# Opening the third attention branch in one stage: the first queries projected between shared keys and values

## The chip, the cores and the metric

The kernel runs on one core of one Trainium2 chip. The metric is the device time of one execution in microseconds (us), as the median of several executions. Beside it stands one profiled execution, from which all rows of the trace come. TensorE (PE) multiplies matrices, VectorE (DVE) and ScalarE (ACT) work elementwise, GpSimd (POOL) does some elementwise work, and the sync engine (SP) issues most DMA transfers.

## The reference

Two blocks run one after the other on 512 tokens of 1024 features, in float32. The first is a transformer block and is not touched. The second has two layers with 256 context tokens beside the 512 latent ones. Each layer projects the normalised input with one wide matrix, runs three attention branches and merges them. The third branch is the one that matters here:

```python
def swa_heads(q, k, v, rope):
    q = q.reshape(b, n, SWA_HEADS, SWA_HD)        # 16 heads of 64
    k = k.reshape(b, n, SWA_KV_HEADS, SWA_HD)     # 4 shared heads of 64
    v = v.reshape(b, n, SWA_KV_HEADS, SWA_HD)
    if rope is not None:
        q = apply_rope(q, *rope)
        k = apply_rope(k, *rope)
    return q, k, v
...
    sq_l, sk_l, sv_l = swa_heads(sq_l, sk_l, sv_l, rope_hd)
    sq_c, sk_c, sv_c = swa_heads(sq_c, sk_c, sv_c, None)
    yc_l = swa_latent(sq_l, sk_l, sv_l, sk_c, sv_c, swa_sink)
```

Queries look at a window of 128 latent tokens to either side and at all context tokens, with a sink term in the softmax. Rope is applied to the latent tokens only. In layer 0 context queries are computed as well, in layer 1 they are not. Then each branch's output is gated and merged.

## The kernel before

Everything is kept feature-major in the on-chip memory: 128 features on the partitions, tokens along the free axis (512 latent, then 256 context). A projection of 128 output features is a *split* product. The weight tile (8 x 128 x 128 values) is loaded in two halves of 256 KB by SP (`load_split`), ScalarE rounds it to a high part (`act_high`, L582), VectorE computes the low part (`dve_low`, L592), and TensorE makes three products for each of 8 input tiles: high by high, high by low and low by high (`split_steps`, `pe_split`; all matrix products go through `mm` and carry line L596). One projection of all 768 tokens is 48 products, one of 512 tokens is 24. Two slots are used in turn for raw, high and low weights; counters on semaphores say which weight is ready. Weight loads are issued by SP in program order, each waiting until its slot's last low part is computed.

`plan()` lists the stages, and each engine goes through them in that order. Between stages each engine calls `fence`: it drains, raises its own fence counter, and waits for the other two engines' counters, unless the stage has a `follower` or is one of some exceptions. A layer of the second block is: norm, `pre`, first branch (`mla`), merge, second branch (`diff`), merge, `swapre`, third branch (`swa`), merge, `out`.

`swapre` opens the third branch. It projects the shared keys (two weights of 128 columns, four key heads) and values (two weights). After each key projection ScalarE (L2403) and VectorE (L2647) copy the results from the accumulator memory to `KB`. After each value projection VectorE copies them to `probs` (L2650). When all four are done, TensorE multiplies the four key tiles with a constant that swaps halves (`rot_hd`, one product each, shown as two records), and then transposes the values (L2251, 12 blocks). VectorE meanwhile turns the keys, four times three operations (`dve_rope`, L1304 to L1307), and then copies the turned values to `v` (L2658). Then comes a fence.

`swa` has 8 steps, one for each pair of query heads. A prologue projects the first pair's queries. ScalarE copies them to `qT` (L1247), SP swaps their halves with four small transfers (`sp_swap`, L447 and L448), GpSimd does the rope on them (`pool_rope`, L1314, L1315, L1317), ScalarE rounds queries and keys (`act_qk_high`, L1270, L1274), VectorE makes their low parts (`dve_qk_low`, L1291, L1295), and only then can TensorE make scores. In each step TensorE makes the scores in groups of two, and between the groups it makes *side* products: the gate projection of this step (`swa_z`) and the next pair's query projection. VectorE takes maxima (L875, L882), ScalarE exponentials (L854), TensorE transposes probabilities and multiplies them with the values, and VectorE scales the result. The next pair's queries pass through the same chain of copy, swap, rope and rounding while the step's values are made.

SP's order in `swa` is written out: the first query weight; then, for each step, the step's gate weight, the next query weight, and the swap of the step's queries.

## Time and profile before

| | us |
|---|---|
| median of 3 runs | 4010.91 |
| lowest and highest run | 4010.6 and 4015.4 |
| profiled execution, its own time | 4009.09 |
| its span, first to last instruction | 4007.3 |
| TensorE busy | 3683.3 |
| VectorE busy | 2044.5 |
| ScalarE busy | 1405.6 |
| GpSimd busy | 257.8 |

The span is what the trace covers, and the profiled execution's own time is 1.8 us longer. Busy times of matrix products are modelled from records, so they are a guide to where an engine works and not to how close it is to its peak. The mean granted clock of TensorE over the span is 0.962, where 1 is 2.4 GHz and 0.5 is 1.2 GHz. In a row of the timeline the first number is the start and the second the duration; a bracket at its end gives how long the engine had been idle and which instruction ended that.

### The profile page before, as it was taken

Reading aid. Unit: us, or ns where it says so; the run is one execution under the profiler, and the core shown is the slowest. Engines: PE = TensorE matmul, PEld = TensorE weight load, DVE = VectorE, ACT = ScalarE, POOL = GpSimd, SP = SyncE. Lnnn points to the kernel's source line nnn. Section 1 sums busy time; section 2 is a strip of 40 time slices with the busy share of each in tenths; the row PEclk is TensorE's granted clock in tenths of the full one; section 3 lists DMA queues with packets and bytes.
Section 4 is the critical chain, followed back from the end, with each engine's and each line's share of the span. In section 5 each row is a group of like instructions: output and inputs, shape, how many; then the busy total and the mean of one; then the engine's idle time right before and its main releaser. Section 6 shows DMA issues by size and latency. Waiting matters only on the chain.

```text
span 4007.3 us, 55652 instructions
## 1 busy us (share of the span) xinstructions
PE 3683.3 (92%) x20467; PEld 2856.3 (71%) x20467; DVE 2044.5 (51%) x3404; ACT 1405.6 (35%) x2502; POOL 257.8 (6%) x196
## 2 busy tenths in 40 slices
PE   5998989999899999999797999989999999798998
PEld 3665778877667787777586777876667777576676
DVE  3565355554445524777623555244552667534644
ACT  2443233323233313444412444122332444414532
POOL 0000000000011001111000110000110112001100
PEclk8999999999899999999898999999999999899999
DMA  7453335542111121211121111211113222121122
GB/s 256 143 144 83 92 102 164 163 136 79 38 29 28 38 63 48 52 47 44 33 62 43 35 40 46 63 53 37 37 39 87 58 65 52 50 74 48 40 73 77
DMA packets 502208, 286.94 MB, mean 72 GB/s; under 512 B 43753, under 2 KB 481093, under 8 KB 502062
## 3 DMA queue, kind: packets, MB, share of 16 engines
q1 hardware_dynamic: 481010, 263.63, 23.5%
q10 hardware_dynamic: 21052, 21.33, 1.7%
q8 instruction: 96, 1.57, 0.2%
q14 instruction: 50, 0.41, 0.0%
HBM read 269.05 MB, written 10.32 MB: 70 GB/s over the span
## 4 chain that ended last, share of the span: by engine, by line
issue 90%; PE 4%; POOL 3%; POOLq 2%; DVE 1%; DVEq 0%; ACT 0%; ACTq 0%
PE ps L596 3%; POOLq L1316 2%; POOL qT L1315 2%; POOL qT L1317 1%; POOL y_and_merged L1315 0%; DVEq L2687 0%; DVE probs L875 0%; PE ps L1022 0%; POOLq L208 0%; DVE y_and_merged L2664 0%; PE ps L2258 0%; DVE y_low L2483 0%; DVE w_low L592 0%; POOL y_and_merged L1317 0%; DVE probs L1928 0%
## 5 line engine op out<-in xcount | busy, mean ns | idle before, releaser
L596 PE MATMUL ps<-h_high,w_high 128*128 128x512 f32 (+1 forms) x3432 | 1287.9, 375 | 75.2 <-DVE w_low L592 24.7
L596 PE MATMUL ps<-h_low,w_high 128*128 128x512 f32 (+1 forms) x3432 | 1252.1, 365 | 0.0
L596 PE MATMUL ps<-h_high,w_low 128*128 128x512 f32 (+1 forms) x3432 | 1248.9, 364 | 0.0
L596 PEld LDWEIGHTS ps<-h_high,w_high 128*128 128x128 f32 x3432 | 655.4, 191 | 238.9 <-issue 97.4
L592 DVE TENSOR_TENSOR w_low<-w_raw,w_high 128x1024 fp32r<-128x1024 f32 x374 | 456.1, 1220 | 629.9 <-ACT w_high L582 607.0
L596 PEld LDWEIGHTS ps<-h_high,w_low 128*128 128x128 f32 x3432 | 656.0, 191 | 104.0
L596 PEld LDWEIGHTS ps<-h_low,w_high 128*128 128x128 f32 x3432 | 657.4, 192 | 92.8 <-issue 1.7
L582 ACT ACTIVATE w_high<-w_raw 128x1024 fp32r<-128x1024 f32 x374 | 387.7, 1037 | 604.6 <-PE ps L596 489.6
L854 ACT ACTIVATE probs<-ps,neg_max 128x768 f32<-128x768 f32 (+1 forms) x240 | 194.5, 814 | 430.2 <-DVE neg_max L886 430.1
L596 PE MATMUL ps<-probsT,v 128*128 128x512 f32 (+4 forms) x736 | 287.3, 560 | 13.5 <-DVE probsT L1085 8.6
L886 DVE TENSOR_REDUCE neg_max<-ps 128x1 f32<-128x768 f32 (+1 forms) x240 | 196.6, 847 | 167.6 <-PE ps L596 156.8
L596 PE MATMUL ps<-k_high,q_high 64*128 64x256 f32 (+4 forms) x784 | 184.5, 394 | 101.6 <-ACT probs L854 30.5
L596 PE MATMUL ps<-y_high,w_high 128*128 128x512 f32 (+1 forms) x640 | 231.5, 362 | 10.1 <-DVE w_low L592 9.2
L596 PE MATMUL ps<-y_low,w_high 128*128 128x512 f32 (+1 forms) x640 | 230.9, 361 | 0.0
L596 PE MATMUL ps<-y_high,w_low 128*128 128x512 f32 (+1 forms) x640 | 230.5, 360 | 0.0
L596 PEld LDWEIGHTS ps<-k_high,q_high 64*128 64x128 f32 (+1 forms) x784 | 91.1, 191 | 172.9 <-ACT probs L854 38.3
L854 ACT ACTIVATE probs<-probs,neg_max 128x512 f32<-128x512 f32 (+1 forms) x192 | 145.6, 758 | 179.4 <-DVE neg_max L878 129.7
L971 PEld LDWEIGHTS ps<-ident,probs 128*128 128x128 f32 x832 | 103.0, 143 | 106.2 <-issue 85.9
L2317 ACT ACTIVATE probs<-ps 128x512 f32<-128x512 f32 x88 | 44.8, 538 | 335.1 <-PE ps L596 335.1
L596 PE MATMUL ps<-y_and_merged 128*128 128x128 f32 (+4 forms) x656 | 153.3, 385 | 8.9 <-DVE y_and_merged L2096 4.6
L1085 DVE COPY probsT<-ps 128x512 f32<-128x512 f32 x112 | 73.2, 654 | 164.1 <-PE ps L971 163.9
L596 PE MATMUL ps<-k_low,q_high 64*128 64x256 f32 (+4 forms) x784 | 156.0, 330 | 0.0
(235 smaller groups left out, 4154.9 us busy)
## 6 DMA issues: line engine op xcount, KB each, us to landing
w_raw<-in_w_in SPq DMA_DIRECT2D x436, 256.0 KB, 3.2
y_and_merged<-in_w_mod SPq DMA_DIRECT2D x96, 256.0 KB, 3.2
w_raw<-in_w_branch SPq DMA_DIRECT2D x96, 256.0 KB, 3.0
w_raw<-in_w_up SPq DMA_DIRECT2D x88, 256.0 KB, 4.3
y_and_merged<-in_w_ada SPq DMA_DIRECT2D x64, 256.0 KB, 3.4
w_raw<-in_w_out SPq DMA_DIRECT2D x48, 256.0 KB, 3.0
w_raw<-in_w_down SPq DMA_DIRECT2D x44, 256.0 KB, 3.0
y_and_merged<-in_w_ada SPq DMA_DIRECT2D x4, 2048.0 KB, 19.7
```

Source lines behind the costliest of these rows:

```text
L582: act.activation(WR[:, k, 0:nk], WRAW[:, k, 0:nk], ACT.Copy).then_inc(s_high, 1)
L592: nc.vector.tensor_tensor(WL[:, k, 0:nk], WRAW[:, k, 0:nk], WR[:, k, 0:nk].bitcast(F32), ALU.subtract).then_inc(s_low, 1)
L596: return nc.tensor.matmul(*a, **kw)
L854: act.activation(it["dst"], src, ACT.Exp, bias=NM[:, idx:idx + 1], accum_out=SL[:, idx:idx + 1]).then_inc(S["exped"], 1)
L886: v.tensor_reduce(NM[:, idx:idx + 1], src, AXX, ALU.max, negate=True).then_inc(S["maxed"], 1)
L971: last = nc.tensor.transpose(PS[:, b:b + 128], tile, ident[:, :])
L1085: nc.vector.tensor_copy(PT[:, which, 0:m], PS[:, b:b + m]).then_inc(S["pt_dve"], 1)
L1315: g.tensor_tensor(x, x, cos, ALU.mult)
L1316: g.drain()
L1317: g.tensor_tensor(x, x, swapped, ALU.add).then_inc(S["roped"], 1)
L2317: last = act.activation(d, p, ACT.Tanh, scale=0.5)
```

## The change

`swapre` gets the third branch as its follower. It projects keys, keys, queries, values, values, instead of keys, keys, values, values, so the first pair's query projection moves from the prologue of `swa` into it. The four key turns are made in two pairs: the products of the first pair stand behind the second key projection, those of the second pair behind the query projection. Their temporary moves, since the swap of the queries now writes the old place. The values use the accumulator banks in another order. The first pair's queries are copied, swapped, turned and rounded inside this stage, and the prologue of `swa` is gone. Because there is a follower, no engine waits at the fence between the two stages. Two semaphores are new: `k_roped`, on which ScalarE waits before it rounds the first keys, and `v_turned`, on which TensorE waits before the first gate projection. SP now loads the first gate weight and swaps the first queries, and then, for each further step, loads the query weight, loads the gate weight and swaps. The number of products, copies and transfers is the same. The same edit removes `prologue()` from TensorE's, ScalarE's and VectorE's part of `swa` (one of the three is shown), and `dve_rope` takes its temporary and its semaphore as arguments.

```diff
@@ -134,8 +134,8 @@
         st += [Stage("merge", name="merge", r=1, subs=1, ctx=cq, l=l)]
-        st += [Stage("swapre", **com)]
-        st += [Stage("units", name="swa", n=8, nh=2, nn=0, subs=1, items=2 * ni, chunks=nc, unroll=1, **com)]
+        swa = Stage("units", name="swa", n=8, nh=2, nn=0, subs=1, items=2 * ni, chunks=nc, unroll=1, **com)
+        st += [Stage("swapre", follower=swa, **com), swa]
         st += [Stage("merge", name="merge", r=2, subs=1, ctx=cq, l=l)]
...
@@ -168,6 +168,9 @@
             n, subs = s["n"], s["subs"]
+            if s["name"] == "swa":
+                s.base["h"] -= 1
+                now["h"] -= 1
             add(s, h=n * s["nh"], n=n * s["nn"], scores=n * subs * s["items"], maxed=n * subs * s["items"],
...
@@ -196,7 +199,7 @@
         elif k == "swapre":
-            add(s, h=4, mm_ev=4, k_out=2, rope_mm=4, roped=4, vt_mm=2)
+            add(s, h=5, mm_ev=4, k_out=2, rope_mm=4, k_roped=4, vt_mm=2, v_turned=2)
     totals = dict(now)
...
@@ -516,13 +519,12 @@
-                        load_split(sp, s, t, 2, 1, cols(win2[l], i * 128 + C_Z + 2048))
                         load_split(sp, s, t, 2, 2, cols(win2[l], i * 128 + (C_SQ + 128)))
-                        sp_swap(sp, s, t, 1, 0)
-                    load_split(sp, s, 0, 2, 0, cols(win2[l], C_SQ))
+                        load_split(sp, s, t, 2, 3, cols(win2[l], i * 128 + (C_Z + 2048 + 128)))
+                        sp_swap(sp, s, t, 1, 1)
+                    load_split(sp, s, 0, 2, 1, cols(win2[l], C_Z + 2048))
+                    sp_swap(sp, s, 0, 1, 0)
                     repeat(sp, 7, 1, body)
-                    load_split(sp, s, 7, 2, 1, cols(win2[l], 7 * 128 + C_Z + 2048))
-                    sp_swap(sp, s, 7, 1, 0)
             elif k == "merge":
...
@@ -561,7 +563,7 @@
             elif k == "swapre":
-                for j, c in enumerate((C_SK, C_SK + 128, C_SV, C_SV + 128)):
+                for j, c in enumerate((C_SK, C_SK + 128, C_SQ, C_SV, C_SV + 128)):
                     load_split(sp, s, 0, 0, j, cols(win2[l], c))
...
@@ -1266,6 +1268,9 @@
             act.wait_ge(S["roped"], cnt(s, "roped", t, s["unroll"] * m, (u + 1) * m))
+            if name == "swa" and i == 0:
+                act.wait_ge(S["k_roped"], s.base["k_roped"])
             rows = slice(0, 96) if name == "mla" else slice(0, 128)
...
@@ -1536,6 +1540,9 @@
                     pe.wait_ge(S["z_ev"], cnt(s, "z_ev", t, 1, u))
+                else:
+                    pe.wait_ge(S["v_turned"], s.base["v_turned"])
                 yield from split_steps(pe, s, t, 2, 1, 128, tgroups(2, s["cq"]))
...
@@ -1649,7 +1656,6 @@
             if name == "swa":
-                prologue()
                 for i in range(7):
...
@@ -2234,22 +2238,27 @@
             elif k == "swapre":
-                for j in range(4):
-                    if j >= 2:
-                        pe.wait_ge(S["mm_ev"], s.base["mm_ev"] + 8 + j - 1)
-                        pe.wait_ge(S["k_out"], s.base["k_out"] + j - 1)
-                    pe_split(pe, s, 0, 0, j, 128, tgroups(2 * (j % 2), True))
-                for g in range(4):
-                    if g == 0:
-                        pe.wait_ge(S["mm_ev"], s.base["mm_ev"] + 8 + 4)
-                    mm(bank(4 + g), TAB["rot_hd"][:, :], KB[:, g, 0:LAT], start=True, stop=True).then_inc(S["rope_mm"], 1)
+                def keys_turned(pair):
+                    pe.wait_ge(S["mm_ev"], s.base["mm_ev"] + 8 + pair + 1)
+                    pe.wait_ge(S["k_out"], s.base["k_out"] + pair + 1)
+                    for g in (2 * pair, 2 * pair + 1):
+                        mm(bank(4 + g), TAB["rot_hd"][:, :], KB[:, g, 0:LAT], start=True, stop=True).then_inc(S["rope_mm"], 1)
+                pe_split(pe, s, 0, 0, 0, 128, tgroups(0, True))
+                pe_split(pe, s, 0, 0, 1, 128, tgroups(2, True))
+                keys_turned(0)
+                pe_split(pe, s, 0, 0, 2, 128, tgroups(0, s["cq"]))
+                keys_turned(1)
+                pe_split(pe, s, 0, 0, 3, 128, tgroups(2, True))
+                pe.wait_ge(S["rope_in"], s["follower"].base["rope_in"] + 1)
+                pe_split(pe, s, 0, 0, 4, 128, tgroups(0, True))
                 for e in range(2):
+                    pe.wait_ge(S["mm_ev"], s.base["mm_ev"] + 8 + 3 + e)
                     for tt in range(6):
-                        last = nc.tensor.transpose(PS[:, 1024 * e + 128 * tt:1024 * e + 128 * tt + 128],
-                                                   PP[:, TOK * e + 128 * tt:TOK * e + 128 * tt + 128], ident[:, :])
+                        last = nc.tensor.transpose(bank(2 - 2 * e, 128, 128 * tt), PP[:, TOK * e + 128 * tt:TOK * e + 128 * tt + 128], ident[:, :])
                     last.then_inc(S["vt_mm"], 1)
...
@@ -2402,6 +2411,13 @@
                         last.then_inc(S["k_out"], 1)
+                    if j == 2:
+                        act.wait_ge(s_h, s.base["h"] + 3)
+                        for d, p in evac_cols(s, 0, Q, s["cq"]):
+                            last = act.activation(d, p, ACT.Copy, scale=0.125)
+                        last.then_inc(S["rope_in"], 1)
+                act_qk_high(act, s["follower"], 0, 0, 0)
...
@@ -2630,32 +2646,53 @@
                 v.drain()
-                dve_rope(dve, s, 0, 0, 1, Q[0:96, 0:LAT], 96, 2, TAB["cos_mla"][:, :], TAB["sin_mla"][:, :])
+                dve_rope(dve, s, 0, 0, 1, Q[0:96, 0:LAT], 96, 2, TAB["cos_mla"][:, :], TAB["sin_mla"][:, :],
+                         PP[0:96, 4608:4608 + LAT], "roped")
                 v.tensor_copy(KH[64:96, :], Q[64:96, :])
                 v.drain()
                 v.tensor_tensor(KL[64:96, :], Q[64:96, :], KH[64:96, :].bitcast(F32), ALU.subtract)
                 dve_latent_inverse(dve, s, 1)
                 dve_latent(dve, s, 1)
             elif k == "swapre":
-                for j in range(4):
-                    dve_low(dve, s, 0, 0, j + 1)
+                def keys(j):
                     dve.wait_ge(s_h, s.base["h"] + j + 1)
-                    b = 1024 * (j % 2)
-                    if j < 2:
-                        for e in range(2):
-                            last = v.tensor_copy(KB[64 * e:64 * e + 64, 2 * j + 1, :], PS[64:128, b:b + TOK])
-                        last.then_inc(S["mm_ev"], 1)
-                    else:
-                        v.tensor_copy(PP[:, TOK * (j - 2):TOK * (j - 1)], PS[:, b:b + TOK]).then_inc(S["mm_ev"], 1)
-                dve.wait_ge(S["k_out"], s.base["k_out"] + 2)
-                v.drain()
-                for g in range(4):
-                    dve_rope(dve, s, g, 0, 1, KB[:, g, 0:LAT], 128, 4 + g, TAB["cos_hd"][:, :], TAB["sin_hd"][:, :])
+                    b = 1024 * j
+                    for e in range(2):
+                        last = v.tensor_copy(KB[64 * e:64 * e + 64, 2 * j + 1, :], PS[64:128, b:b + TOK])
+                    last.then_inc(S["mm_ev"], 1)
+                def turn_keys(pair):
+                    dve.wait_ge(S["k_out"], s.base["k_out"] + pair + 1)
+                    v.drain()
+                    for g in (2 * pair, 2 * pair + 1):
+                        dve_rope(dve, s, g, 0, 1, KB[:, g, 0:LAT], 128, 4 + g, TAB["cos_hd"][:, :], TAB["sin_hd"][:, :],
+                                 PP[:, 2 * TOK:2 * TOK + LAT], "k_roped")
+                def values(e):
+                    dve.wait_ge(s_h, s.base["h"] + 4 + e)
+                    b = 1024 - 1024 * e
+                    v.tensor_copy(PP[:, TOK * e:TOK * e + TOK], PS[:, b:b + TOK]).then_inc(S["mm_ev"], 1)
+                dve_low(dve, s, 0, 0, 1)
+                keys(0)
+                dve_low(dve, s, 0, 0, 2)
+                keys(1)
+                dve_low(dve, s, 0, 0, 3)
+                turn_keys(0)
+                dve_low(dve, s, 0, 0, 4)
+                turn_keys(1)
+                values(0)
+                dve_low(dve, s, 0, 0, 5)
+                dve_qk_low(dve, s["follower"], 0, 0, 0)
+                values(1)
                 for e in range(2):
                     dve.wait_ge(S["vt_mm"], s.base["vt_mm"] + e + 1)
-                    v.tensor_copy(VB[:, :, 128 * e:128 * e + 128], PS[:, 1024 * e:1024 * e + TOK].rearrange("p (a d) -> p a d", d=128))
+                    b = 1024 - 1024 * e
+                    v.tensor_copy(VB[:, :, 128 * e:128 * e + 128], PS[:, b:b + TOK].rearrange("p (a d) -> p a d", d=128)).then_inc(S["v_turned"], 1)
             elif k == "store":
```

## Rows read from the trace of the kernel before

**Rows 1.** The page, parts 1 and 6 (median us to landing last)

```profile
PE 3683.3 (92%) x20467; PEld 2856.3 (71%) x20467; DVE 2044.5 (51%) x3404; ACT 1405.6 (35%) x2502; POOL 257.8 (6%) x196
...
w_raw<-in_w_in SPq DMA_DIRECT2D x436, 256.0 KB, 3.2
```

**Rows 2.** Timeline of TensorE, opening in layer 0

```profile
2117.51 0.47 PE L596 MATMUL ps<-h_high,w_high 128*128 128x512 f32 x1 [2.64 <-DVEq L2687]
...
2152.16 3.27 PE L596 MATMUL ps<-y_and_merged,rot_hd 128*128 128x512 f32 x7 [1.05 <-DVE probs L2650]
...
2155.70 1.47 PE L2251 MATMUL ps<-ident,probs 128*128 128x128 f32 x12
...
2163.89 0.76 PE L596 MATMUL ps<-h_high,w_high 128*128 128x512 f32 x1 [6.71 <-DVEq L2687]
...
2186.47 0.58 PE L596 MATMUL ps<-k_high,q_high 64*128 64x256 f32 x2 [12.22 <-DVE k_low L1295]
```

**Rows 3.** Timeline of TensorE, a merge's projection and the opening in layer 1

```profile
3547.82 0.39 PE L596 MATMUL ps<-h_high,w_high 128*128 128x512 f32 x1
...
3553.26 0.39 PE L596 MATMUL ps<-y_high,w_high 128*128 128x512 f32 x1
...
3560.90 0.47 PE L596 MATMUL ps<-h_high,w_high 128*128 128x512 f32 x1 [2.04 <-DVEq L2687]
...
3595.55 3.70 PE L596 MATMUL ps<-y_and_merged,rot_hd 128*128 128x512 f32 x8 [1.05 <-DVE probs L2650]
...
3607.27 0.76 PE L596 MATMUL ps<-h_high,w_high 128*128 128x512 f32 x1 [6.71 <-DVEq L2687]
...
3626.50 0.58 PE L596 MATMUL ps<-k_high,q_high 64*128 64x256 f32 x2 [11.53 <-DVE k_low L1295]
```

**Rows 4.** Stretches: PE, PEld, DVE, ACT, POOL, clock, DMA share, GB/s

```profile
2117.40:2151.00 33.60, 33.49 (x192) 29.60 (x192) 9.70 (x9) 7.47 (x8) 0.00 (x0) 1.00 0.24 64
...
2163.80:2174.30 10.50, 10.35 (x48) 8.75 (x48) 1.23 (x1) 1.08 (x2) 0.00 (x0) 0.82 0.00 0
...
2186.40:2190.00 3.60, 3.54 (x17) 2.93 (x18) 1.71 (x8) 0.85 (x3) 0.00 (x0) 0.50 0.02 5
```

**Rows 5.** Timeline of VectorE, layer 0

```profile
2153.33 0.69 DVE L1304 TENSOR_TENSOR y_and_merged<-y_and_merged,cos_hd 128x512 f32<-128x512 f32 x1 [1.22 <-PE ps L596]
...
2161.93 1.82 DVE L2658 COPY v<-ps 128x768 f32<-128x768 f32 x2
```

**Rows 6.** Timeline, the first queries of layer 0

```profile
2174.28 0.87 ACT L1247 ACTIVATE qT<-ps 128x512 f32<-128x512 f32 x2 [9.35 <-PE ps L596]
...
2179.06 1.26 POOL L1314 TENSOR_TENSOR probs<-probs,sin_hd 128x512 f32<-128x512 f32 x1 [266.67 <-DMA probs<-qT]
...
2182.97 0.84 ACT L1270 ACTIVATE q_high<-qT 128x768 fp32r<-128x768 f32 x1 [7.83 <-POOL qT L1317]
...
2185.46 0.95 DVE L1295 TENSOR_TENSOR k_low<-y_and_merged,k_high 128x768 fp32r<-128x768 f32 x1
```

**Rows 7.** Timeline, steps of the branch in layer 0

```profile
2216.83 1.27 POOL L1314 TENSOR_TENSOR probs<-probs,sin_hd 128x512 f32<-128x512 f32 x1 [33.89 <-DMA probs<-qT]
...
2261.96 0.39 PE L596 MATMUL ps<-k_high,q_high 64*128 64x256 f32 x2
...
2290.09 1.27 POOL L1314 TENSOR_TENSOR probs<-probs,sin_hd 128x512 f32<-128x512 f32 x1 [33.10 <-DMA probs<-qT]
```

**Rows 8.** Timeline, second step of the branch in layer 1

```profile
3648.47 0.95 SPq L372 DMA_DIRECT2D w_raw<-in_w_in  x2
...
3653.91 1.04 ACT L582 ACTIVATE w_high<-w_raw 128x1024 fp32r<-128x1024 f32 x1
...
3657.46 0.72 ACT L854 ACTIVATE probs<-probs,neg_max 128x512 f32<-128x512 f32 x1 [2.50 <-DVE neg_max L878]
```

**Rows 9.** Timeline, VectorE beside GpSimd in the second branch

```profile
1730.38 1.94 DVE L592 TENSOR_TENSOR w_low<-w_raw,w_high 128x1024 fp32r<-128x1024 f32 x1
...
1731.19 2.28 POOL L1315 TENSOR_TENSOR qT<-qT,cos_hd 128x512 f32<-128x512 f32 x1
```

More of the change, by code:

```diff
@@ L148, in plan @@
     keys = ("h n square added square_mm rstd scaled high low_row lat_sq lat_ss lat_rs lat_ri lat_sp lat_n rinv spread fin down_ev x_t mm_ev rope_in rope_mm roped q_mm k_mm k_out q_out kv_ev kv_low vt_in vt_mm v_ev z_ev tanh swap_q swap_k z_scaled scores maxed exped normed "
-            "pt_act pt_dve rl_mm transposed o_done o_sq o_ss o_rs y bias merged up_ev gelu f_high f_low y_low y_high y_round m_high m_low out_ev ctx_in mod_copy mod_sum qk_high qk_low").split()
+            "k_roped v_turned pt_act pt_dve rl_mm transposed o_done o_sq o_ss o_rs y bias merged up_ev gelu f_high f_low y_low y_high y_round m_high m_low out_ev ctx_in mod_copy mod_sum qk_high qk_low").split()
     for k in keys:
@@ L1296, in dve_qk_low, with dve_rope @@
             last.then_inc(S["qk_low"], 1)
-        def dve_rope(dve, s, key_off, t, per, x, rows, b, cos, sin):
+        def dve_rope(dve, s, key_off, t, per, x, rows, b, cos, sin, tmp, done):
             dve.wait_ge(S["rope_mm"], cnt(s, "rope_mm", t, per, key_off + 1))
             v = nc.vector
-            tmp = PP[0:rows, 4608:4608 + LAT]
             v.tensor_tensor(x, x, cos, ALU.mult)
@@ L1306, in dve_rope @@
             v.drain()
-            v.tensor_tensor(x, x, tmp, ALU.add).then_inc(S["roped"], 1)
+            v.tensor_tensor(x, x, tmp, ALU.add).then_inc(S[done], 1)
             v.drain()
@@ L1768, in act_units @@
             if name == "swa":
-                prologue()
                 for i in range(7):
@@ L1856, in dve_units @@
             if name == "swa":
-                prologue()
                 for i in range(7):
@@ L2395, in act_stage @@
             elif k == "swapre":
-                for j in range(4):
+                for j in range(5):
                     act_high(act, s, 0, 0, j + 1)
```

1 line of the change is left out of this document (removed).

## The prediction

> **What bounds the kernel now.** I read the page first. TensorE is busy 92% of the span [rows 1], so time can only be won where it stands still or runs at the lower of its two clock levels. The timeline of TensorE then gives the two openings of the third branch, one per layer [rows 2, 3]. The first number of a row is its start and the bracket is the idle time before it, with its releaser. In layer 0 TensorE starts the first key projection at 2117.51, waits 1.05 us for VectorE's eviction of the last values, runs the rope products and the twelve transposes, waits 6.71 us at the fence, projects the first queries, waits 12.22 us for `k_low`, and starts the first scores at 2186.47. Layer 1 has the same picture with 1.05, 6.71 and 11.53 us. These six waits are 39.3 us together. The stretch view adds the clock: while the first queries are projected the granted clock is 0.82, and in the 3.6 us from 2186.40 it is 0.50, which is 1.2 GHz [rows 4]. In the 6.71 us VectorE makes four key turns from 2153.33 to 2161.93 (8.60 us, so 2.15 each), then two value copies of 1.82 us together [rows 5]. The first queries have a chain of their own [rows 6]: eviction at 2174.28, four copies by the DMA queue, GpSimd from 2179.06, ScalarE's rounding at 2182.97, VectorE's last `k_low` at 2185.46 for 0.95 us. It is a chain of small steps in which TensorE does nothing.
>
> **What the change does to TensorE's path, layer 0.** Before, from the first key product to the first score: 2186.47 - 2117.51 = 68.96 us [rows 2]. After, the same stretch is this sum.
> - Five projections instead of four ahead of the transposes. Four took until 2152.16 - 1.05 = 2151.11, so 33.60 us, 8.40 each. Five are 42.00 us. All stand back to back.
> - Eight rope records: 2155.70 - 2152.16 = 3.54 us, now in two halves of 1.77, with no wait. The first half needs the first keys' evictions, which ran while the second keys were projected, and the second half needs evictions that run beside the query projection.
> - The tail. Six transposes of the first values take 1.47 / 2 = 0.74 us, inside the 1.05 us that the last values' eviction takes. The other six follow, 0.74. So 1.05 + 0.74 = 1.79 us after the last projection.
> - The seam into the first scores. The stage has a follower, so the fence is passed with a drain and no wait. No row shows a drain alone. Below it is bounded by nothing, above by the 2.64 us of a whole fence at this stage's entry [rows 2]. A drain must only empty TensorE's own queue, so I take 0.2 us.
>
> Sum 42.00 + 3.54 + 1.79 + 0.20 = 47.53, against 68.96: 21.43 us won.
>
> **Layer 1.** Before: 3626.50 - 3560.90 = 65.60 us [rows 3]. Here the queries have 512 columns and no context. A projection of that size takes 3553.26 - 3547.82 = 5.44 us for its 24 products at the high clock, where it took 7.7 us after the fence. After: 4 x 8.40 + 5.44 + 3.54 + 1.79 + 0.20 = 44.57. Won: 21.03 us.
>
> **The clock after the opening.** The first step of the branch starts at 1.2 GHz. From the first score to GpSimd's next rope it takes 2216.83 - 2186.47 = 30.36 us, and the third step, which does the same work, takes 2290.09 - 2261.96 = 28.13 us [rows 2, 7]. After the change TensorE comes to the first scores out of 42 us of products. The 2.64 us of idleness at the entry left the granted clock at 1.00, 2.4 GHz, in the 33.6 us behind it [rows 4]. So 2.23 us a layer, 4.46 for both. I use layer 0's difference for layer 1 too.
>
> **What the sum rests on: who must be in time.** Let T be the end of the query projection.
> - The queries' chain. Eviction to the end of GpSimd's work is 2182.97 - 2174.28 = 8.7 us [rows 6], so it ends at T + 8.7. The values' first projection ends at T + 1.77 + 8.40 = T + 10.2. ScalarE rounds the next weight first, so `q_high` starts at about T + 11.2, and from `q_high` to `k_low`'s end before was 2186.41 - 2182.97 = 3.4 us, which gives T + 14.6. VectorE evicts the second values behind `k_low`, and these end at T + 18.6. So `k_low` has 4.0 us to spare, and GpSimd 2.5 us more ahead of `q_high`.
> - The keys' turns. VectorE turns two keys (4.3 us) while the queries are projected and two in the first values' projection, after one weight split at about T + 3.4, so they end by T + 7.8. That is ahead of the values' eviction at T + 10.2. This work was the larger part of the 6.71 us. It is hidden only as long as a projection is longer than it.
> - The new wait on `v_turned` stands ahead of the first gate projection, because that writes the banks that the value copies read. Behind it on TensorE are all side products of the first step and the second pair of scores. VectorE's copies start when the last eviction ends and end 1.05 + 1.82 = 2.87 us after the last projection. The first scores start at 1.99. The wait is at most 0.88 us a layer and at least nothing. One pair of scores fills most of that gap, so I take 0.1 each, 0.2 in all.
> - The sync queue. The first swap now stands behind one weight load whose slot is free when the first values' weight is split, during the query projection, so it is not held. In the loop the next head's query weights are now loaded behind the swap instead of ahead of it. In layer 1's second step the queue is free for loads at 3648.47, a 256 KB half takes 3.2 us to land [rows 1], so both halves are there at about 3652.5. ScalarE's first rounding after that is at 3653.91, and it stands ahead of the first exponential at 3657.46 [rows 8]. A rounding started by 3656.4 still costs nothing, so there are some 4 us to spare in each of 14 steps. I take 0.
>
> **Total.** 21.43 + 21.03 + 4.46 - 0.20 = 46.7 us. The profiled execution took 4009.09 us, with a span of 4007.3. It becomes 3962.4. The median of the runs is 4010.91, 1.8 above, so 3964.2.
>
> **A price that could spoil the cover.** GpSimd's rope now runs beside VectorE's key turns and evictions. The trace has such a meeting: in the second branch GpSimd's product took 2.28 us and VectorE's weight split beside it 1.94 [rows 9], where GpSimd alone takes 1.26 [rows 6]. Three products at 2.28 instead of 1.26 are 3.1 us late. That is 0.6 us more than GpSimd's own 2.5 and far within the 4.0 of `k_low`. The sum stays. The Trainium skill (GPSIMD Engine Reference, Key points) says that GpSimd shares its SBUF interfaces with VectorE and collides with VectorE instructions that have two SBUF inputs, as the two key-turn products here have. The rows agree in kind. If each engine in turn stood still for the other, it would be the second rival, at 3971.2.
>
> **Rivals.**
> - The clock stays low or falls again. The transposes and short waits before the first score are thin work. For: 6.71 us of idleness did bring it down [rows 4]. Against: 1.05 and 2.64 us did not. If the first step is still slow, 4.46 us are not won: 3968.6. Chance 0.06.
> - The queries' chain ends last, through the collision above. For: GpSimd's slow product [rows 9]. Against: it was one in three, and VectorE's turns are over before GpSimd is. Were each of its three products twice 2.28 us long, it would end 9.9 us later, at T + 18.6. With 3.4 for rounding, 1.79 for the tail and 0.2 for the seam the first score comes at T + 24.0 instead of T + 20.5: 3.5 us a layer, 3971.2. Chance 0.05.
> - The fence does not go in effect: TensorE waits at the seam as long as now, 6.71 us in each layer, because VectorE's turns, split around other work, end late. For: VectorE's order is now rigid, and a late weight split delays the turn behind it. Against: the times above. 3964.2 + 13.4 = 3977.6. Chance 0.04.
> - Slower than before: the query weights behind the swap come too late in every step. ScalarE then holds the first exponential, and the step's chain of exponentials behind it, 14 times. For: two full weights now queue at once. Against: landing takes 3.2 us and 4 us are free. It would take 46.7 / 14 = 3.3 us past the margin, a landing of some 10.5 us, from which on the kernel is slower; a landing of 11 us gives 3964.2 + 14 x 3.9 = 4019. A milder lateness of 1 us past the margin gives 3978. Chance 0.05, of it 0.03 slower and 0.01 within the bound.
>
> **How the numbers follow.** My forecast has 0.80. Its own range comes from the seam (-0.4 to +4.9 us for both layers), the `v_turned` wait (-0.2 to +1.6) and the runs' spread of about 2: 3960 to 3972. The range for 8 in 10 takes in the clock rival and the collision, and part of the milder lateness: 3958 to 3976. A change of 0.2% is 8 us, about what a measurement of this kernel can tell from none. All cases but the last one's tail are faster by more than that: faster 0.95, same 0.02, slower 0.03.
>
> **What would show it.** TensorE has no idle time over 1 us between the entry of the stage and the first scores, and the granted clock stays 1.00. From the first key product to the first score it is about 47.5 us in layer 0 and 44.6 in layer 1. Rope products stand in two groups, GpSimd's first rope lies under the first values' projection. From the first score to the next rope is about 28.1 us in layer 0. The other steps keep their pitch. The prediction is wrong if a `v_turned` or `k_low` wait of several us appears, or if the steps grow because ScalarE waits for a weight.

## The result, and the profile after

| | before | after |
|---|---|---|
| median, first comparison (4 runs each) | 4010.76 us | 3969.02 us |
| lowest and highest run | 4009.74 and 4015.4 | 3961.84 and 3975.22 |
| ratio of the times, 95% interval | | 0.9889 [0.9878, 0.9901] |
| profiled execution, its own time | 4009.09 | 3967.67 |
| its span | 4007.3 | 3965.9 |

The kernel became 1.1% faster. The forecast of 3964.2 is a ratio of 0.9884, inside the interval. The same kernel run a second time gave 0.9891 [0.9876, 0.9907].

The timeline of TensorE at the opening in layer 0 answers to [rows 2]. First column the start, second the duration, bracket the idle time before and its releaser:

```profile
2120.63 0.47 PE L598 MATMUL ps<-h_high,w_high 128*128 128x512 f32 x1 [2.64 <-DVEq L2724]
...
2137.39 1.88 PE L598 MATMUL ps<-y_and_merged,rot_hd 128*128 128x512 f32 x4
...
2147.45 1.88 PE L598 MATMUL ps<-y_and_merged,rot_hd 128*128 128x512 f32 x4
...
2167.07 0.88 PE L2261 MATMUL ps<-ident,probs 128*128 128x128 f32 x6 [0.40 <-DVE probs L2677]
...
2168.23 0.39 PE L598 MATMUL ps<-k_high,q_high 64*128 64x256 f32 x2 [0.29 <-issue]
```

The rope products stand in two groups without a wait. Between the entry and the first scores TensorE is idle for 0.40 + 0.29 us, where it was 20 us. From the first key product to the first score it is 2168.23 - 2120.63 = 47.60 us. Layer 1, which answers to [rows 3]:

```profile
3542.99 0.47 PE L598 MATMUL ps<-h_high,w_high 128*128 128x512 f32 x1 [2.05 <-DVEq L2724]
...
3586.60 0.88 PE L2261 MATMUL ps<-ident,probs 128*128 128x128 f32 x6 [0.40 <-DVE probs L2677]
...
3587.73 0.39 PE L598 MATMUL ps<-k_high,q_high 64*128 64x256 f32 x2 [0.26 <-issue]
```

Here it is 44.74 us. The stretches of layer 0 (busy time of PE, PEld, DVE, ACT, POOL, then granted clock, DMA share, GB/s) answer to [rows 4]:

```profile
2150.00:2166.00 16.00, 16.00 (x96) 14.20 (x95) 9.96 (x11) 2.53 (x3) 4.80 (x3) 1.00 0.31 78
2166.00:2172.00 6.00, 5.31 (x37) 4.05 (x34) 5.41 (x10) 2.69 (x5) 0.00 (x0) 1.00 0.01 3
2172.00:2176.00 4.00, 4.00 (x25) 3.30 (x25) 2.04 (x7) 1.54 (x3) 0.00 (x0) 1.00 0.00 0
```

The clock is 1.00 through the opening and into the first step. GpSimd's rope (4.80 us) now lies under the first values' projection. The chain of the first queries, in order, answers to [rows 6]; VectorE's key turns are beside it:

```profile
2147.65 0.87 ACT L2418 ACTIVATE qT<-ps 128x512 f32<-128x512 f32 x2 [7.36 <-PE ps L598]
...
2152.49 1.54 POOL L1318 TENSOR_TENSOR probs<-probs,sin_hd 128x512 f32<-128x512 f32 x1 [237.00 <-DMA probs<-qT]
...
2152.97 1.61 DVE L1308 TENSOR_TENSOR y_and_merged<-y_and_merged,cos_hd 128x512 f32<-128x512 f32 x1
...
2153.99 1.74 POOL L1319 TENSOR_TENSOR qT<-qT,cos_hd 128x512 f32<-128x512 f32 x1
...
2155.25 1.03 DVE L1311 TENSOR_TENSOR y_and_merged<-y_and_merged,probs 128x512 f32<-128x512 f32 x1
2155.87 1.56 POOL L1321 TENSOR_TENSOR qT<-qT,probs 128x512 f32<-128x512 f32 x1
...
2158.74 0.83 ACT L1275 ACTIVATE q_high<-qT 128x768 fp32r<-128x768 f32 x1
...
2161.21 0.95 DVE L1300 TENSOR_TENSOR k_low<-y_and_merged,k_high 128x768 fp32r<-128x768 f32 x1
```

The chain ends at 2162.16, and its product is needed at 2168.23. The first step from score to rope, which answers to [rows 7]:

```profile
2196.39 1.28 POOL L1318 TENSOR_TENSOR probs<-probs,sin_hd 128x512 f32<-128x512 f32 x1 [38.96 <-DMA probs<-qT]
```

2196.39 - 2168.23 = 28.16 us, the length of a later step.

**The account of the profiled execution.** The opening is the stretch from the first key product to the first score. The openings became 68.96 - 47.60 = 21.36 and 65.60 - 44.74 = 20.86 us shorter. The first steps became 30.36 - 28.16 = 2.20 us shorter in layer 0 and 2.49 in layer 1 (22.92 against 20.43). Together this is 46.9 us. The execution became 41.4 us shorter. The first opening starts 3.1 us later than before (2120.63 against 2117.51), though nothing ahead of it was changed. From one opening's start to the next it is 1422.36 us, against 1443.39 before, so 21.0 less where 23.6 had been won: another 2.5 us. The experiments look for these 5.5 us too.

### The profile page after: what moved, and what is told of

Same layout as the page of the kernel before. It is cut to its first block, busy times and chain, and to the rows that moved or that the text cites. A ratio compares the mean times of both kernels' runs of the same rounds, so it can differ in the third digit from the quotient of the medians.

```text
span 3965.9 us, 55654 instructions
## 1 busy us (share of the span) xinstructions
PE 3678.2 (93%) x20467; PEld 2849.7 (72%) x20467; DVE 2047.2 (52%) x3404; ACT 1405.5 (35%) x2502; POOL 260.0 (7%) x196
## 4 chain that ended last, share of the span: by engine, by line
issue 90%; PE 4%; POOL 3%; POOLq 2%; DVE 1%; DVEq 0%; ACT 0%; ACTq 0%
PE ps L598 4%; POOLq L1320 2%; POOL qT L1319 2%; POOL qT L1321 1%; POOL y_and_merged L1319 0%; DVEq L2724 0%; DVE probs L877 0%; PE ps L1024 0%; PE ps L2267 0%; POOLq L211 0%; DVE y_low L2499 0%; DVE y_and_merged L2701 0%; DVE w_low L594 0%; POOL y_and_merged L1321 0%; DVE probs L1932 0%
```

## The experiments

The kernels were measured in three groups, each with its own runs of the kernel before. In the first group are the changed kernel again, the inner fence back, the queries last and the first of the two entry kernels (nine runs of the kernel before, median 4012.26 us). In the second are the queries fourth, the two kernels on the sync queue and the kernel before again (17 runs, 4013.08). In the third are the two shifted kernels, the second entry kernel and the one with both entries (19 runs, 4012.14). Medians are compared within a group and ratios across groups. Distances within the stages come from each kernel's own profile. There the openings of one code agree to 0.3 us, with one exception: the second opening of the kernel with the sync queue's old order.

**The changed kernel again**, no edit.

> The changed kernel, unchanged. Theory A (the 5 us that are missing from the forecast of 46.7 are lost ahead of and between the two openings, where nothing was changed, in stretches after waits of 3 to 5 us in which TensorE's clock falls in one execution and not in another): in this profile the openings again take 47.6 us (layer 0) and 44.7 us (layer 1) from the first key product to the first score, the start of the first opening moves by one or more us against 2120.6, and the runs spread over some 10 us around a median between 3962 and 3970. Theory B (the change itself costs the 5 us, somewhere in the third branch): the start of the first opening stays at 2120.6 and the runs agree within 3 us.

3969.72 us (3967.01 to 3973.6). Openings of 47.57 us (2122.64 to 2170.21) and 44.73 us (3545.19 to 3589.92). The first opening starts at 2122.64, two us later than in the first profile. So the openings repeat to 0.03 us, and what lies ahead of them does not. From one opening's start to the next it is 1422.55 us against 1422.36, so the 2.5 us lost between them did not come back. On the openings and the start this is theory A. The spread of 6.6 us is less than it said, and where the clock fell is a matter of its own (last section).

**The inner fence back.**

```diff
-            if s["follower"] is not None:
+            if s["follower"] is not None and s.kind != "swapre":
                 return
```

> The changed kernel with the fence between the two stages back. Theory A (what was won is the work moved under projections; the fence was only the place where its end was waited for): TensorE waits for VectorE's two value copies, which end 2.9 us after the last projection instead of 1.8 for the last transpose, so the openings grow by 0.9 to 1.5 us each, 48.5 to 49.1 and 45.6 to 46.2 us, and the time by 2 to 3 us. Theory B (leaving out the fence is what pays): 6.7 us come back in each layer, openings of 54.3 and 51.4 us, the time 13 us longer.

3974.9 us, ratio 0.9905 [0.9889, 0.992]. The entry and the first score in this kernel's timeline:

```profile
2118.01 0.47 PE L598 MATMUL ps<-h_high,w_high 128*128 128x512 f32 x1 [2.64 <-DVEq L2724]
...
2166.45 0.39 PE L598 MATMUL ps<-k_high,q_high 64*128 64x256 f32 x2 [1.14 <-DVEq L2724]
```

The openings are 48.44 and 45.60 us. The fence costs 1.14 us of idleness instead of 0.26, 0.87 us a layer in all. Its 6.71 us of before were not its price but that of the key turns and value copies waited for there. The median is 5.2 us above that of the changed kernel in the same group, and the openings explain 1.7 of it; the intervals overlap. The openings lie 0.06 us and less under the bounds of theory A and nearly 6 us under those of theory B. Theory A.

**Queries last.** The diff shows TensorE's part. Weights, banks and waits moved accordingly, and VectorE's low parts of queries and keys now stand behind its value copies. There it waits 7.57 us for ScalarE's `k_high` first, so their place costs nothing.

```diff
                 keys_turned(0)
-                pe_split(pe, s, 0, 0, 2, 128, tgroups(0, s["cq"]))
+                pe_split(pe, s, 0, 0, 2, 128, tgroups(0, True))
                 keys_turned(1)
                 pe_split(pe, s, 0, 0, 3, 128, tgroups(2, True))
-                pe.wait_ge(S["rope_in"], s["follower"].base["rope_in"] + 1)
-                pe_split(pe, s, 0, 0, 4, 128, tgroups(0, True))
+                pe.wait_ge(S["mm_ev"], s.base["mm_ev"] + 8 + 3)
+                pe_split(pe, s, 0, 0, 4, 128, tgroups(0, s["cq"]))
```

> The changed kernel with the order keys, keys, values, values, queries: no fence, key turns in pairs as changed, but nothing behind the queries' projection except the transposes. Theory A (the place between keys and values hides the queries' chain): the chain of 12.2 and 11.5 us stands bare again, openings of 57.8 and 54.2 us, and the first step starts at 1.2 GHz and takes 2.2 us more to the next rope; in all 22 to 25 us slower than the changed kernel. Theory B (the fence and the key turns made up most of the gain): less than 10 us slower.

3992.46 us, ratio 0.9944 [0.9931, 0.9958], 22.7 us above the changed kernel of the same group. Its timeline of TensorE and the clock of the stretches before and after the first score:

```profile
2182.83 0.58 PE L598 MATMUL ps<-k_high,q_high 64*128 64x256 f32 x2 [10.45 <-DVE k_low L1300]
```

```profile
2171.00:2183.00 12.00, 1.25 (x10) 0.81 (x9) 3.74 (x4) 3.09 (x5) 3.74 (x3) 0.68 0.41 109
2183.00:2190.00 7.00, 7.00 (x30) 5.44 (x32) 2.77 (x7) 1.63 (x4) 0.00 (x0) 0.58 0.01 2
```

Openings 57.67 and 53.99 us, 10.1 and 9.3 more than in the changed kernel. TensorE waits 10.45 us for `k_low`, and the clock is down again when it starts. From the first score to the next rope it is 30.94 us (2182.83 to 2213.77) instead of 28.16. Theory A: of the 46.9 us in openings and first steps some 23 are the place of the queries. About as much is the rest: the key turns under projections, the fence and the clock of the query projection. No run parts these three, except that the fence alone is 0.87 us a layer.

**Queries fourth**, between the two values.

```diff
-                for j, c in enumerate((C_SK, C_SK + 128, C_SQ, C_SV, C_SV + 128)):
+                for j, c in enumerate((C_SK, C_SK + 128, C_SV, C_SQ, C_SV + 128)):
...
-                dve_qk_low(dve, s["follower"], 0, 0, 0)
                 values(1)
...
+                dve_qk_low(dve, s["follower"], 0, 0, 0)
```

The other engines' orders, banks and waits moved accordingly. The last lines are a second difference: VectorE makes the low parts behind the last values' eviction and the two value copies, not ahead of them.

> The changed kernel with the order keys, keys, values, queries, values: one projection less ahead of the first score behind the queries. Theory A (the queries' chain takes 8.7 us to the end of GpSimd's work and 3.4 for rounding and low parts, 12.1 us, and is hidden only by what stands behind the query projection): 8.4 us of projection, 1.8 of tail and the seam hide 10.4 of 12.1 us, so each opening grows by 1.5 to 2.5 us, to 49.1 to 50.1 and 46.2 to 47.2 us. Theory B (the chain has ample room, and any place ahead of the last projection does): openings as in the changed kernel, 47.6 and 44.7 us.

3976.37 us, ratio 0.9905 [0.9888, 0.9922]. Openings of 50.10 us (2117.75 to 2167.85) and 46.93 us (3547.50 to 3594.43), 2.5 and 2.2 more.

```profile
2164.05 2.01 DVE L2695 COPY v<-ps 128x768 f32<-128x768 f32 x2
...
2164.42 0.83 ACT L1279 ACTIVATE k_high<-y_and_merged 128x768 fp32r<-128x768 f32 x1
...
2166.84 0.95 DVE L1300 TENSOR_TENSOR k_low<-y_and_merged,k_high 128x768 fp32r<-128x768 f32 x1
2167.85 0.58 PE L598 MATMUL ps<-k_high,q_high 64*128 64x256 f32 x2 [2.78 <-DVE k_low L1300]
```

Theory A by the numbers, at its upper end. With one projection behind the queries TensorE waits 2.78 us in layer 0 and 2.52 in layer 1. But not all of this is the chain. `k_high` is there at 2165.25 and VectorE starts `k_low` at 2166.84, since its value copies stand ahead of the low parts here. An estimate from these rows: with the low parts first, `k_low` could come 1.6 us earlier, and about 1.2 of the 2.78 us would be left. The wait has a second price. The granted clock in the 3.4 us behind it is 0.51, and from the first score to the next rope it takes 29.66 and 21.93 us instead of 28.16 and 20.43. The two projections behind the queries in the changed kernel hide the chain with room.

**The sync queue's old order in the steps.**

```diff
-                        load_split(sp, s, t, 2, 2, cols(win2[l], i * 128 + (C_SQ + 128)))
-                        load_split(sp, s, t, 2, 3, cols(win2[l], i * 128 + (C_Z + 2048 + 128)))
-                        sp_swap(sp, s, t, 1, 1)
...
+                    load_split(sp, s, 0, 2, 2, cols(win2[l], C_SQ + 128))
+                    with sp.Fori(1, 7) as t:
+                        load_split(sp, s, t, 2, 1, cols(win2[l], t * 128 + C_Z + 2048))
+                        load_split(sp, s, t, 2, 2, cols(win2[l], t * 128 + (C_SQ + 128)))
+                        sp_swap(sp, s, t, 1, 0)
```

> The changed kernel with the sync queue's old order in the steps: the next query weight is loaded ahead of the step's swap again. Theory A (the weight behind the swap lands in time): the steps keep their distance from rope to rope, 36.3 us from the second to the third in layer 0 and 26.8 us in layer 1, and the time stays. Theory B (a part of the missing 5 us is ScalarE waiting for that weight): the steps become shorter, by 0.3 us or more each.

3976.83 us, ratio 0.9898 [0.9879, 0.9916]: not faster. The seven distances from rope to rope in layer 0 are 263.74 us together, against 264.02 in the second profile of the changed kernel. In layer 1 the first two full distances are 26.88 and 29.69 us, against 26.80 and 28.12. The longer one is a clock matter, as the stretches show, this kernel first, then the second profile of the changed one:

```profile
3612.60:3639.40 26.80, 26.01 (x174) 18.17 (x173) 15.65 (x38) 13.55 (x29) 3.73 (x3) 1.00 0.19 50
3639.40:3669.10 29.70, 27.53 (x174) 19.22 (x174) 16.52 (x39) 14.28 (x30) 3.77 (x3) 0.94 0.17 45
```

```profile
3610.40:3637.20 26.80, 26.07 (x174) 18.23 (x173) 15.63 (x38) 13.55 (x29) 3.77 (x4) 1.00 0.19 50
3637.20:3665.30 28.10, 26.00 (x174) 18.24 (x173) 16.51 (x39) 14.28 (x30) 3.75 (x4) 1.00 0.18 47
```

The same 174 products take 1.5 us more where the granted clock is 0.94. Theory A: the load behind the swap costs nothing.

The second opening of this kernel is 46.29 us and not 44.7 as in every other kernel with this order of products and no fence in it. The entry, and the clock behind it:

```profile
3545.78 0.67 PE L599 MATMUL ps<-h_high,w_high 128*128 128x512 f32 x1 [2.05 <-DVEq L2725]
```

```profile
3545.70:3549.00 3.30, 3.22 (x8) 2.58 (x9) 1.23 (x1) 1.06 (x1) 0.00 (x0) 0.53 0.03 5
```

In the changed kernel the same first 3.3 us hold 14 products at a clock of 1.00. So idleness of 2.05 us at the entry was followed by the lower level in this profile and not in the others. The prediction took from one row that the entry's idleness leaves the clock up. That holds in most profiles, not in all.

**That load held back.**

```diff
+                        sp.wait_ge(S["qk_low"], cnt(s, "qk_low", t, 1, 1))
                         load_split(sp, s, t, 2, 2, cols(win2[l], i * 128 + (C_SQ + 128)))
```

> The changed kernel, with the query weight's load in each step held until the step's queries have their low parts, about 6 us later than the swap. Theory A (lateness of this weight past the margin of some 4 us holds ScalarE's first exponential and lengthens every step one for one): the weight lands about 2.5 us too late, the 14 steps grow by 2 to 3 us each, 28 to 42 us slower than the changed kernel. Theory B (TensorE has side products in that time, so that ScalarE's lateness is partly hidden): less than 1 us a step, under 14 us slower.

3981.89 us, ratio 0.9921 [0.9904, 0.9938]. Neither theory as written. The load is issued 7.0 to 9.2 us behind the swap instead of 0.5, so it is 6.5 to 8.6 us later (11 us at the first swap of each layer). In layer 0 the seven distances are 264.33 us together, 0.3 more than in the changed kernel, although ScalarE waits for the weight there too. In layer 1 they are 215.17 against 200.73: 14.4 us more, 2.1 a step. TensorE's busy time in them grows by 4.6 us (196.60 against 192.01) for the same 1254 products, at a mean clock of 0.98 instead of 1.00, and its idle time by 9.9. So a third of the price is the clock behind longer waits. ScalarE in layer 1, with the queue's issue ahead of it:

```profile
3646.41 2.13 SPq L375 DMA_DIRECT2D w_raw<-in_w_in  x4
```

```profile
3650.30 1.06 ACT L585 ACTIVATE w_high<-w_raw 128x1024 fp32r<-128x1024 f32 x1 [5.75 <-DMA w_raw<-in_w_in]
```

ScalarE waits for the weight, which is there 3.9 us after the issue. So a late weight does lengthen the steps of layer 1. In the changed kernel ScalarE waits for no weight in any of these steps, so there is a margin. Its size, which the prediction put at some 4 us, is not measured: only one lateness was tried.

**The kernel before again**, no edit.

> The kernel before, unchanged, for a second profile. Theory A (the unchanged code around the openings differs from one execution to the next by where the clock falls): the openings take 68.96 and 65.60 us again, and the start of the first opening (2117.5 in the first profile) and the distance from the layer's `out` stage to the second opening (945.5) move by one us or more. Theory B (the changed kernel's later starts, 2118.0 to 2125.2 in five profiles, come from the change): 2117.5 and 945.5 come again within 0.5 us.

4014.3 us, ratio 1.0002 [0.9993, 1.0011]. Openings 68.68 us (2118.39 to 2187.07) and 65.59 us (3561.24 to 3626.83). The first opening starts 0.9 us later than in the first profile, and the distance from the `out` stage to the second opening is 945.46, the same. The distance answers to theory B. The start moved by 0.88 us, which lies between the bounds of the two theories and decides nothing.

**The kernel before, shifted** by extra products in layer 0, 3 and 8 of them.

```diff
             elif k == "swapre":
+                for _ in range(3 if l == 0 else 0):
+                    mm(bank(4), ident[:, :], XT[:, 0, :], start=True, stop=True)
```

> The kernel before, with three extra products (identity by one tile of 512 columns, into a bank that is free there) ahead of the first key projection of layer 0; they change no result. They shift all later work by about 1.4 us. Theory A (where the clock falls behind a wait hangs on when the work comes, and the change shifts it by 23 us): the distance from the layer's `out` stage to the second opening, 945.5 us in both profiles of the kernel before and 946.0 to 951.8 in seven profiles of changed kernels with the same code there, moves off 945.5 by one us or more. Theory B (the changed code makes that stretch longer): 945.5 again.

> As the kernel with three extra products, with eight: a shift of about 3.7 us. Theory A: the same distance moves off 945.5 here or with three. Theory B: 945.5 in both.

Ratios 1.0013 [1.0003, 1.0022] for both. The distances are 945.64 and 945.51 us, so theory A failed here, with these two shifts. The start of the opening itself moved, ahead of the extra products: 2121.62 with three, 2117.70 with eight. The code ahead of it is that of the kernel before, where it was 2117.51 and 2118.39. So a start 3 us later needs no change of code.

The shifts were not those that were meant. The openings became 71.86 and 75.46 us, so the products cost 2.9 and 6.5 us and not 1.4 and 3.7. With the starts that came along, layer 0's `out` stage begins at 2622.48 and 2621.74, where it began at 2615.41 and 2615.78. Both kernels moved layer 1 by 6 to 7 us, so they are nearly one trial. With eight products the seven distances from rope to rope in layer 1 are 196.54 us, against 194.36 and 194.34 in the kernel before, so unchanged steps can become longer under the old opening too.

**TensorE not waiting at the entry**, twice.

```diff
+            if me == "pe" and s.kind == "merge" and s["r"] == 1:
+                return
...
+                pe.wait_ge(S["tanh"], s.base["tanh"])
                 pe_split(pe, s, 0, 0, 0, 128, tgroups(0, True))
+                pe.wait_ge(S["merged"], s.base["merged"])
                 pe_split(pe, s, 0, 0, 1, 128, tgroups(2, True))
```

> The changed kernel, and TensorE does not wait at the fence ahead of the opening either: it waits only for the last gate evaluation before the first key projection and for the last merged tile before the second, whose banks these free. Theory A (TensorE's idle 2.64 and 2.05 us at the entry are only the fence): both become less than 0.3 us, 4.2 us faster than the changed kernel, which lies inside the spread of single runs and shows in the profile. Theory B (ScalarE and VectorE are the ones that are late, with the second key weight, since they still wait at the fence): the idle time moves to the second key projection, nothing is won.

> The changed kernel with TensorE not waiting at the fence ahead of the opening, once more. Theory A (2.4 and 1.8 us of idleness are gone): a median 4.2 us under the changed kernel's 3969.4, 3963 to 3967, and 0.3 us of idleness at each entry. Theory B (the 5.8 us by which its median was lower were chance): 3969 or more.

3963.88 and 3962.43 us, ratios 0.9875 [0.986, 0.989] and 0.9872 [0.9856, 0.9889]. The second one's timeline:

```profile
2120.73 0.47 PE L598 MATMUL ps<-h_high,w_high 128*128 128x512 f32 x1 [0.26 <-issue]
...
3540.53 0.47 PE L598 MATMUL ps<-h_high,w_high 128*128 128x512 f32 x1 [0.26 <-issue]
```

Theory A: 2.4 and 1.8 us of idleness are gone, and the openings keep their 47.6 and 44.7 us, so no wait has moved to the second key projection. The first median is 5.8 us under that of the changed kernel in its group. The intervals of the ratios overlap, so the profile shows this gain more surely than the times do.

**The same at the entry of the second branch too.**

```diff
-            if me == "pe" and s.kind == "merge" and s["r"] == 1:
+            if me == "pe" and s.kind == "merge" and s["r"] in (0, 1):
...
+                if not ahead and name == "diff":
+                    pe.wait_ge(S["tanh"], s.base["tanh"])
                 yield from split_steps(pe, s, t, s["nh"], 0, 128, tgroups(0, cq))
+                if not ahead and name == "diff":
+                    pe.wait_ge(S["merged"], s.base["merged"])
```

> As that kernel, and the same at the entry of the second branch: TensorE waits for the last gate evaluation before its first query projection and for the last merged tile before its first key projection. Theory A: the 2.25 and 1.78 us of idleness there become 0.3, 3.4 us faster than with the third branch's entry alone, 3960 to 3963. Theory B (the second weight is then late, since ScalarE and VectorE still wait at the fence): the idle time moves to the key projection.

3958.81 us (3957.63 to 3962.41), ratio 0.9866 [0.985, 0.9883], 3.6 us under the third branch's entry alone in the same group. The second branch's first products:

```profile
1501.84 0.47 PE L598 MATMUL ps<-h_high,w_high 128*128 128x512 f32 x1 [0.26 <-issue]
...
3051.23 0.47 PE L598 MATMUL ps<-h_high,w_high 128*128 128x512 f32 x1 [0.26 <-issue]
```

Theory A: 5.22 and 4.69 us of waiting for `w_low` stand further on in the stage here, and 5.23 and 4.71 with the third branch's entry alone, so nothing moved there. In layer 0 the clock gains as well. With the fence and its 2.24 us of idleness the first product takes 0.77 us, and it is 32.00 us to the product behind the wait for `w_low`; without them 0.47 and 30.47 us. This is the version with the lowest median, and its interval overlaps that of the version before it.

## Why the prediction was right

- **The sum of each opening** was forecast at 47.53 and 44.57 us and came out at 47.60 and 44.74. The five projections, the rope products in two groups and the tail of 1.05 + 0.74 us came as costed. The seam was put at 0.2 us and shows 0.29 and 0.26.
- **The clock after the opening** gave 2.20 us in layer 0, forecast 2.23, and 2.49 in layer 1.
- **The queries' chain.** With T = 2147.6, GpSimd ended at T + 9.8 instead of T + 8.7, `q_high` began at T + 11.1 (forecast 11.2), and `k_low` ended at T + 14.6 as forecast. The queries-fourth kernel shows that one projection is not enough: 2.8 us stand bare, of which some 1.6 are VectorE's own order there.
- **The keys' turns** ended at T + 8.7 instead of T + 7.8, ahead of the values' eviction at T + 10.1. The prediction places all four turns, 8.60 us, in the old wait of 6.71 us. That wait began at 2157.2, so 4.8 us of turns and both value copies lie in it. The sum does not hang on this.
- **The collision** happened. GpSimd's three products took 1.54, 1.74 and 1.56 us instead of some 1.26, and VectorE's key-turn product 1.61 instead of 0.69. It cost 1.1 us on GpSimd's part of the chain, which had 2.5 to spare, so nothing on the path. By the rule of the Trainium skill (GPSIMD Engine Reference, Key points) it is the products with two SBUF inputs that meet GpSimd; the two that grew, L1308 and L1311, are of that kind, and L1309, which reads the accumulator, stayed at 0.68. The rows also suggest how the price arises. L1308 began at 2152.97 beside a product of GpSimd that ended at 2154.03. Its plain 0.69 us behind that would end at 2154.72, and it ended at 2154.58. GpSimd's third product began at 2155.87 beside L1311, which ended at 2156.28. Its plain 1.26 us behind that would end at 2157.54, and it ended at 2157.43. So each looks like a wait for the other's end and then the plain time. No run tests this. The prediction named that case and priced it as its second rival, with products of twice 2.28 us. Here VectorE's products are 0.69 us long, and so the waits were short.
- **The wait on `v_turned`** was put at 0.1 us a layer. No idle time of 0.15 us or more stands there.
- **The sync queue's order** was costed at nothing. The old order brought no time back, and a load held back by 6.5 to 8.6 us cost 2.1 us a step in layer 1 alone. In the slower rival the price was one us for one us in 14 steps. That was too high for layer 0, where the late weight cost nothing.
- **The total.** The forecast of 46.7 us met 46.9 us in the two openings and first steps of the profiled execution, and 41.4 us in its whole. The medians of the first comparison differ by 41.7 and those of the second by 42.5. The interval of the second, 0.9876 to 0.9907, is 37 to 50 us of 4012, so 46.7 is not excluded. Of the 5.5 us missing in the profiled execution, 3.1 lie ahead of the first opening, where kernels with the old opening differ by 4.1 us among themselves. The other 2.5 lie between the openings and stay open (below). The forecast had no term for either: it took everything outside the openings and first steps as unchanged. So it was right on what was moved and some 5 us too high on the whole.

The rivals did not come in the changed kernel. The clock rival came in a small way beside it: a second opening of 46.29 us in the kernel with the old order. The fence, had it stayed, costs 0.87 us a layer and not 6.71, because the work that was waited for had moved.

## What to carry to other kernels

A long wait at a fence is often the price of the work that ends there. Move that work under products first; then the fence itself was worth 0.9 us here. When a small serial chain (copy, transfers, rope, rounding) stands between a product and its consumer, add up its pieces and put that many us of independent products behind the product: 12 us were hidden by two projections of 8.4, and one left 2.8 us bare. Look too at what stands ahead of the chain's last piece on its own engine, which was some 1.6 of these 2.8 us. An engine that needs only two banks freed can wait for these instead of for a whole stage, which took away another 2.4 and 1.8 us of idleness.

## What the runs showed of the hardware that was not expected

TensorE's granted clock fell where the trace shows it busy without a gap. In the changed kernel's profile, in layer 1's first stages, which the change does not touch:

```profile
2710.35:2713.35 3.00, 3.00 (x28) 3.00 (x27) 0.36 (x1) 0.31 (x1) 0.00 (x0) 1.00 0.33 103
2713.35:2716.35 3.00, 3.00 (x24) 2.87 (x24) 1.15 (x4) 1.80 (x3) 0.00 (x0) 1.00 0.02 5
2716.35:2719.35 3.00, 3.00 (x9) 2.38 (x9) 0.80 (x1) 0.00 (x0) 0.00 (x0) 0.58 0.35 76
2719.35:2722.35 3.00, 3.00 (x13) 2.38 (x12) 0.00 (x0) 0.00 (x0) 0.00 (x0) 0.85 0.33 99
2722.35:2725.35 3.00, 3.00 (x26) 2.96 (x25) 0.00 (x0) 0.00 (x0) 0.00 (x0) 1.00 0.00 0
```

The same stretch in the kernel before:

```profile
2737.00:2740.00 3.00, 3.00 (x14) 2.44 (x14) 0.79 (x1) 0.00 (x0) 0.00 (x0) 1.00 0.33 73
2740.00:2743.00 3.00, 3.00 (x20) 2.71 (x19) 0.00 (x0) 0.00 (x0) 0.00 (x0) 1.00 0.34 102
```

TensorE is busy 3.00 of 3.00 us ahead of the fall and in it, at 2.4 GHz before and near 1.2 GHz in it, and the stretch takes 1.6 us longer. But busy is not the same work throughout. This one lies in the first two rows:

```profile
2712.78 2.74 PE L598 MATMUL ps<-ones,probs 128*128 128x2 f32 x24
```

These are 24 products of 2 columns each, and until 2715.38 TensorE does nothing else. The clock falls 1.4 us later. Ten profiles have the changed opening or a variant of it. In nine of them the clock falls at this place, 0.1 to 1.4 us behind these products. The tenth, with the queries last, and the four with the old opening have the same 24 products and no fall there. So the products alone do not explain it, and it is open what else is needed. The Trainium skill (TensorE: Matmul & The Clock Gate, What's actually happening) says that activity releases the throttle and idleness brings it back. The rows do not settle whether this stretch agrees, since the busy time counts a product of 2 columns like any other.

The distance from the start of layer 0's `out` stage to the second opening, with this stretch in it, was 945.5 to 945.6 us in four profiles of kernels with the old opening. It was 948.2 and 947.2 in two profiles of the changed kernel, 950.8 with the inner fence back, 951.8 with the queries fourth, 950.9 with the old order, 947.4 with the load held back, and 946.0 with the queries last. The code in it is the same in all of these. In the three kernels with changed entries, which save 1.8 us or more inside it, it was 945.4 to 945.8. Set beside the kernel before, product by product, the changed kernel loses 1.5 of its 2.7 us at the fall above and about 0.5 us in each of two later places. The two shifted kernels, nearly one trial, did not bring the fall. So what ties it to the changed kernels is open, and with it 2.5 of the 46.7 us. The forecast took the clock of unchanged stretches as unchanged. That did not hold here, nor in the steps of layer 1: distances of 28.1 us from rope to rope in the changed kernel are 29.6 us in several other profiles, one of them of a kernel with the old opening.
